# Two orders of work in a two-block layer kernel: the norms' sums and spread one product later, the second gate's work behind level 4's operands

## The reference

```python
def first_block(x, ...):
    h = _rmsnorm(x, norm_mix[layer])
    x = x + _hgrn2_mixer(h, w_in, lb, out_norm, w_out)
    x = x + _squared_relu_mlp(_rmsnorm(x, norm_mlp[layer]), mlp_w1[layer], mlp_w2[layer])
    return _rmsnorm(x, norm_final)

# in _hgrn2_mixer, 8 heads of 128:
    o = _hgrn2_chunk_scan(heads(qf), heads(k), heads(i), heads(log_f))
    o = o * lax.rsqrt(jnp.mean(o * o, axis=-1, keepdims=True) + NORM_EPS)
    o = o.reshape(b, s, D_MODEL) * out_norm * jax.nn.silu(g)
    return o @ w_out

def second_block(x, ...):
    h = x + hybrid_mixer(rms_norm(x, norm1_g), w_in, conv_w, conv_norm_g, ret_norm_g, w_out)
    h = h + sq_relu_mlp(rms_norm(h, norm2_g), w_up, w_down)
    return rms_norm(h, final_norm_g)

# in hybrid_mixer, 4 retention heads of 128:
    q = rotary(rq.reshape(b, s, RET_HEADS, RET_HEAD_DIM), positions)
    k = rotary(rk.reshape(b, s, RET_HEADS, RET_HEAD_DIM), positions) * (RET_HEAD_DIM ** -0.5)
    o = chunkwise_retention(q, k, v).reshape(b, s, RET_WIDTH)
```

## Time and profile before

| | us |
|---|---|
| median of the runs (3) | 2459.65 |
| lowest, highest | 2459.26, 2460.57 |
| the profiled execution | 2461.4 |
| its span, first to last instruction | 2459.6 |
| TensorE matmul busy in the span | 2430.9 (99%) |
| VectorE busy | 991.5 (40%) |
| GpSimd busy | 895.9 (36%) |
| ScalarE busy | 447.3 (18%) |

### The profile page before, as it was taken

One profiled execution on the slowest core, in us unless ns is written; L12 is line 12 of the kernel. 1 busy time (PEld: TensorE's weight loads), 2 busy tenths in 40 slices (PEclk: granted clock), 3 DMA queues, 4 the chain that ended last, 5 costly groups with the idle time before them and its releaser, 6 DMA issues.

```text
span 2459.6 us, 30077 instructions
## 1 busy us (share of the span) xinstructions
PE 2430.9 (99%) x11520; PEld 2034.6 (83%) x11520; DVE 991.5 (40%) x1361; ACT 447.3 (18%) x723; POOL 895.9 (36%) x1020
## 2 busy tenths in 40 slices
PE   7999999999999999999999999999999999999998
PEld 6888888888888888888888888888888888888886
DVE  5667676754211212212355656454321221221224
ACT  4233233422201201101230002002220110110210
POOL 3322223343433433433442324453433333333342
PEclk9999999999999999999999999999999999999999
DMA  4110111121111111111111111111111111111112
GB/s 146 35 35 27 35 34 35 49 89 60 43 52 51 43 51 51 43 51 50 45 51 60 35 43 43 43 43 52 43 51 45 50 51 43 51 51 43 51 52 77
DMA packets 36647, 123.17 MB, mean 50 GB/s; under 512 B 4704, under 2 KB 4832, under 8 KB 36576
## 3 DMA queue, kind: packets, MB, share of 16 engines
q1 hardware_dynamic: 35568, 120.54, 15.8%
q10 hardware_dynamic: 1008, 1.62, 0.2%
HBM read 117.95 MB, written 4.19 MB: 50 GB/s over the span
## 4 chain that ended last, share of the span: by engine, by line
PE 97%; DVE 2%; DVEq 1%; issue 0%; DMA 0%; ACT 0%; SPq 0%; ACTq 0%
PE prod_ps L400 30%; PE prod_ps L402 30%; PE prod_ps L401 30%; PE side_ps L536 2%; PE side_ps L453 2%; PE side_ps L459 1%; PE side_ps L477 1%; PE side_ps L467 1%; PE side_ps L469 1%; DVE x_res L1353 0%; PE side_ps L486 0%; DVE sq_sum L819 0%; DVEq L919 0%; DMA x_in<-x_t 0%; DVEq L1081 0%
## 5 line engine op out<-in xcount | busy, mean ns | idle before, releaser
L400 PE MATMUL prod_ps<-operand_hi,w_hi 128*128 128x512 f32 x3264 | 1286.2, 394 | 12.6 <-POOL w_lo L347 9.3
L402 PE MATMUL prod_ps<-operand_hi,w_lo 128*128 128x512 f32 x3264 | 1274.4, 390 | 0.0
L401 PE MATMUL prod_ps<-operand_lo,w_hi 128*128 128x512 f32 x3264 | 1273.0, 390 | 0.0
L343 POOL CAST w_hi<-w_raw 128x1024 fp32r<-128x1024 f32 x200 | 211.2, 1056 | 1486.0 <-PE prod_ps L402 1480.8
L400 PEld LDWEIGHTS prod_ps<-operand_hi,w_hi 128*128 128x128 f32 x3264 | 614.7, 188 | 139.4 <-POOL w_lo L347 9.3
L402 PEld LDWEIGHTS prod_ps<-operand_hi,w_lo 128*128 128x128 f32 x3264 | 614.1, 188 | 129.9
L401 PEld LDWEIGHTS prod_ps<-operand_lo,w_hi 128*128 128x128 f32 x3264 | 614.9, 188 | 123.5
L347 POOL TENSOR_TENSOR w_lo<-w_raw,w_hi 128x256 fp32r<-128x256 f32 x800 | 666.5, 864 | 16.0
L1099 DVE SCALAR_TENSOR_TENSOR work<-prod_ps,inv_rms 128x512 f32<-128x512 f32 x128 | 88.4, 692 | 492.2 <-PE prod_ps L402 491.6
L1594 ACT ACTIVATE work<-work 128x512 f32<-128x512 f32 x128 | 81.0, 633 | 1042.0 <-DVE work L1099 1042.0
L1111 DVE TENSOR_TENSOR x_res<-prod_ps,x_res 128x512 f32<-128x512 f32 x96 | 66.4, 692 | 442.5 <-PE prod_ps L402 442.5
(11 more groups left out here) (150 smaller groups left out, 1109.8 us busy)
## 6 DMA issues: line engine op xcount, KB each, us to landing
w_raw<-stream SPq DMA_DIRECT2D x204, 512.0 KB, 3.6
x_in<-x_t SPq DMA_DIRECT2D x16, 256.0 KB, 7.0
x_res<-x_t SPq DMA_DIRECT2D x8, 512.0 KB, 4.6
out_t<-x_res SPq DMA_DIRECT2D x16, 256.0 KB, 2.1
masks_f<-masks SPq DMA_DIRECT2D x1, 896.0 KB, 9.6
ret_rows<-head_rows ACTq DMA_DIRECT2D x1, 512.0 KB, 3.5
ret_cos<-rope ACTq DMA_DIRECT2D x1, 512.0 KB, 4.5
ret_sin<-rope ACTq DMA_DIRECT2D x1, 512.0 KB, 5.2
```

The source lines that it names most:

```text
L343: nc.gpsimd.tensor_copy(w_hi[:, slot], w_raw[:, slot]).then_inc(high_made, 1)
L400: nc.tensor.matmul(prod_ps[:, bank], w_h, a_h, start=(k == 0), stop=False)
L401: nc.tensor.matmul(prod_ps[:, bank], w_h, a_l, start=False, stop=False)
L402: last = nc.tensor.matmul(prod_ps[:, bank], w_l, a_h, start=False, stop=(k == KT - 1))
```

## The change

On TensorE the two sums move from between the first two products of the second input projection into the middle of the second product, and both spreads from the middle of the second into the middle of the third. On VectorE, in the gates' iterations 8 and 9, `second(1)` and `third(1)` move from around `group(2)` to behind level 3, and a drain is added behind `third(0)`. On ScalarE `gate_high(1)` moves from ahead of `gate_sigmoid(2)` and the fourth gather to behind them.

```diff
+            def both_sums():
+                norm_sums(T_NORM2, 3)
+                norm_sums(T_NORM2 + 1, 3, flat_sum_g)
+
             def both_norms():
                 pe.wait_ge(rms_paired, 1)
                 norm_spread(T_NORM2 + 2, HEADS1 + 3, 1)
                 spread((T_NORM2 + 3) % 2)
...
                 product(u, s0, 0, 0, count, mid=old("v"))
-                if first:
-                    norm_sums(T_NORM2, 3)
-                    norm_sums(T_NORM2 + 1, 3, flat_sum_g)
-                else:
+                if not first:
                     ret_old(n - 1, "kv")
-                product(u, s0, 1, 0, mid=both_norms if first else None)
+                product(u, s0, 1, 0, mid=both_sums if first else None)
                 if not first:
                     ret_old(n - 1, "o")
-                product(u + 1, s1, 0, 0)
+                product(u + 1, s1, 0, 0, mid=both_norms if first else None)
                 product(u + 1, s1, 1, 0)
...
                 if gates_now:
                     second(0)
                     third(0)
+                    dve.drain()
                 if older:
 
                     step = hgrn_step(n, "T")
                     turned = done_step(step).rearrange("p (c t) -> p c t", c=NB)
                     nc.vector.tensor_copy(h_s[par][:, 1::2], turned[:, 1::2]).then_inc(taken(step), 1)
-                second(1)
+                if not gates_now:
+                    second(1)
                 group(2)
-                third(1)
+                if not gates_now:
+                    third(1)
                 newer_level(3)
+                if gates_now:
+                    second(1)
+                    third(1)
                 newer_level(4)
...
             gather(1, prev, 3)
             gate_high(0)
-            gate_high(1)
             gate_sigmoid(2)
             gather(1, prev, 4)
+            gate_high(1)
             take_o(HEADS1)
```

## The result

The changed kernel takes 2462.51 us (median of 20 runs, 2460.71 to 2464.09) where the kernel before takes 2459.62 (20 runs beside it, 2457.91 to 2461.36). The ratio is 1.0013, with a 95% interval of 1.0007 to 1.0019: 2.9 us slower. The prediction said 2458.7 us, 2455.8 to 2461.6. The direction was wrong, and the median lies 0.9 us above the range.

What follows compares the result with a forecast made beforehand. TensorE, busy 2430.9 of 2459.6 us, was taken as the bound. Gate moves' 1.2 us plus the sums' and spreads' -0.2 took 1.0 off the profiled 2461.4, giving 2460.4; the median 1.75 lower, 2458.7, range 2455.8 to 2461.6.

Steps and rivals of the forecast that it cites:

- VectorE's chains: Gates, iteration 8: VectorE starts level 4 0.6 us earlier and is 1.2 us ahead from level 5.
- part 1: The VectorE and ScalarE moves in the gates: worth 1.2 us, bounds 0 and 2.4.
- The new wait at level 6: Iteration 8: TensorE waits 2.2 us for ScalarE's gather, without a clock fall, and reaches `back` 1.2 us earlier.
- the slower rival: Clock falls at every new gap: twice in the sums (3.4 us), at `scores` (1.4), at level 6; 2461.2 us, 13%.
- The spread and the double set of sums: Second input projection: sums start without a wait, spread at 1309.1 against 1310.41, 1.3 us earlier, before clock loss.
- I take one fall: Clock loss in the two adjacent sets of sums: one fall, 1.7 us, priced from the fall at level 4.
- The wait at `scores`: TensorE waits 3.9 us for VectorE's chain, 19.35 us from the spread; the clock falls there, costing 1.4 us.
- The slack before: At `scores` in the old kernel, TensorE's work from the spread exceeded VectorE's chain by 1.6 us.
- The way from the profiled execution to the median: The profiled execution's 1.75 us above the median was subtracted unchanged, turning 2460.4 into 2458.7 us.
- Full recovery: Rival at both places: VectorE's chains don't bind, 10.7 us is won, giving 2449 us; chance 7%.

Runs made afterwards that it cites:

- e8: The kernel before, unchanged, profiled a second time as a single execution; 2457.73 us.
- e3: Against part 2 alone, the second set of sums stands behind the second product, not next to the first set; 2459.32 us.
- part 2 alone: Also e2: the kernel before with only TensorE's changed order of sums and spreads, VectorE and ScalarE as before; 2461.75 us, ratio 1.0010.
- v_best: e6 joined with part 1 and the gates of products 3 to 5 moved later; 2450.18 us, ratio 0.9965 to the kernel before.
- e10: The changed kernel, unchanged, profiled a second time as a single execution; 2461.37 us.
- e4: Against part 2 alone, TensorE does the first head's scores inside the product behind it, half a product later; 2458.13 us.
- e5: Part 2 alone with the edits of both e3 and e4; 2455.11 us, ratio 0.9986 to the kernel before.
- e6: e5 with VectorE's multiplication for `ret_q_xi` moved behind `scores`; 2453.42 us, ratio 0.9977 to the kernel before.

## Why the prediction was wrong, step by step

**VectorE's chains: right.** Level 4 was to start 0.6 us earlier and level 5 1.2. From `o`, level 4 started at 7.38 us before (426.72 - 419.34) and 6.79 after, level 5 at 14.91 and 13.63: 0.6 and 1.3. The rows laid beside it as an analogue, those with the same distance to POOL's cast, gave the right size. But most of that lead was the clock's: in e8, the kernel before without the fall, level 4 starts at 6.91 us from `o` (425.08 - 418.17) and level 5 at 13.76, so that against it part 1 brings 0.1 us at either. The Trainium skill's rule on the shared port pair (SBUF — State Buffer, "SBUF: two separate sides") fits level 3's small product: it took 1.12 us beside the cast, and the one of the same shape in iteration 7 of the trace before took 0.28 (at 368.82). The two moved gate instructions were only lengthened to 0.90 and 1.07 us (two of the same shape at 427.84 and 428.67, with POOL idle, took 0.75 and 0.69), beside four of POOL's that took 3.71: neither stood for a whole one of these, as the prediction had read the rule.

**The new wait at level 6: right in place, 1.92 us for 2.2; wrong in its consequence.** The sum had `back` 1.2 us earlier with no fall, 20.15 us behind `o`. Without a fall that is what came, 20.01. But three of four profiles with part 1 have the fall, which was kept for the slower rival, and then it is 20.99. Compared like with like, part 1 gives 0.15 us without falls and 0.35 with them. The 1.2 us was the difference between an execution with a fall (before) and a forecast one without (after).

**The spread and the double set of sums: the step that failed.** "I take one fall", 1.7 us, was the term. The clock came down in the second set, at 1301.4, and stayed down until 1308.2, 6.8 us where the fall at the first place, from which the price was taken, lasted 3.4, and the spread stood 13.65 us behind the last addition where one fall would have given 12.0. That is 1.65 us at the spread, handed on in full to `scores` (33.03 us behind the last addition, forecast 31.4). The rival that took two falls there, 3.4 us, had the right size. e3 shows the cause: with the two sets apart the clock doesn't fall, and the spread stands 3.6 us earlier than in part 2 alone. So the term was 3.6 us, not 1.7.

**The wait at `scores`: right.** 3.84 us for 3.9, and 19.4 us from spread to `scores` for 19.35. The fall behind it costs 1.7 us in the profile, not 1.4: from `scores` to the turn of k it is 8.93 us, and 7.24 in the trace before. (The slack before was 1.5 us rather than 1.6: in TensorE's timeline `scores` starts at 1331.24, the 1331.40 being that of the chain's row.)

**The way from the profiled execution to the median: wrong, and as large as the falls.** The execution before lay 1.75 us above its median, and this was carried over unchanged. Its second and third profiles show where such an excess comes from: against e8 it lost 1.2 us ahead of `o`, 1.2 at place 1 and 1.45 at place 2. The last two are at the very places that the change rebuilds. So the sum took full credit for falls that only a part of the executions of the kernel before have (four of eight profiles at place 1, the long one at place 2 in two of six), and then subtracted them a second time, in part, as an offset. The changed kernel's profiled execution lies 0.1 us under its own median, not 1.75 above it. In the sum: the changed kernel's profiled execution came 2.0 us above the 2460.4 forecast for it (2.1 at place 2, 0.85 at place 1, less 0.6 by which it was early at `o` and 0.2 behind place 2), and its median 3.8 above the 2458.7, the other 1.8 being the offset.

**Full recovery** didn't happen with this change. Its 10.7 us were near what both places hold, though: v_best has 8.9 of them, but only with the later steps moved too.

**Still open:** why a fall comes behind 1.92 or 2.24 us of idle time in some executions and not in others, and what in the double set brings it. The single moving column, the loads and the 0.26 us between the sets were never varied alone; moving the sets apart changes how much nearly empty work stands together and takes that 0.26 us away as well. The runs show how often and at what cost, not the rule.

## What to carry to other kernels

A wait moved off the busiest engine is worth only the slack of the next step that waits for the same partner engine; add up that engine's chain to each later meeting point, and move those steps too, or the gain stands there as a new wait. Small steps that leave the matmul engine nearly empty cost most here where they stood together: try them spread among dense work. And when one profiled execution lies above the median, find the excess in it before using it, since it may sit in the very place that the change is to mend.

## What the runs showed of the hardware that was not expected

Two sets of 16 one-column matmuls with their weight loads, back to back with 0.26 us between them and no idle time over that, bring TensorE's clock from its higher to its lower level (1.00 to 0.50) in all four profiles of the double set (after, e10, e2, e4), and the second set then takes 3.0 to 3.2 us for 1.84. The same sets 4.6 us apart (their starts) leave it at 1.00 in all four profiles of that order (e3, e5, e6, v_best). The weight loads didn't keep the clock up: they were busy for 2.82 of the 3.40 us up to 1300.9, just ahead of the fall, and for 3.21 of the 3.40 behind it. The same 2.24 us of idle time was followed by a fall in four of eight profiles, at a cost of 1.2 us by the next step that VectorE sets. And the same kernel's profiled executions differ for such reasons: 21.35 or 20.15 us for one stretch, 39.70 or 38.25 for another.
